# Scores of a latent-attention head in one product of 96 rows, the first projection by pairs of input chunks, and the last output tile by halves

## The reference

```python
h = h + 0.5 * SwiGLU_1(RMSNorm(h))            # width 2816
z = RMSNorm(h) @ w_in                         # 1824 columns
a = u * (W_s v + b)                           # chunk MLP
b = sliding-window attention with sinks       # 8 query heads, 2 key heads
c = latent attention, 4 heads                 # below
h = h + concat(a, b, c) @ w_out
h = h + 0.5 * SwiGLU_2(RMSNorm(h))
```

```python
s = q_nope . k_nope + q_pe . k_pe             # 64 terms + 32 terms, per head
p = softmax(s * (64 + 32) ** -0.5)            # masked by chunks of 64
```

## Time and profile before

| what | value |
|---|---|
| median of three runs | 2032.96 us |
| the profiled execution's own time | 2033.12 us |
| its span, first to last instruction | 2031.3 us |
| mean granted TensorE clock | 0.996 |
| PE busy | 2013.7 us, 99% |
| DVE, ACT, POOL busy | 1665.6, 972.5, 356.6 us |
| DMA over the span | 175.40 MB, 86 GB/s |

### The profile page before, as it was taken

How to read it: one execution, slowest core, us unless ns; L and a number is a source line. 1 busy time by engine, 2 the same in 40 slices (tenths; PEclk the granted TensorE clock), 3 DMA queues, 4 the chain that set the end, 5 groups by cost and what they waited for, 6 DMA issues and landing times.

```text
span 2031.3 us, 40732 instructions
## 1 busy us (share of the span) xinstructions
PE 2013.7 (99%) x15315; PEld 1961.2 (97%) x15315; DVE 1665.6 (82%) x2456; ACT 972.5 (48%) x1768; POOL 356.6 (18%) x218
## 2 busy tenths in 40 slices
PE   8999999999999999999999999999999999999998
PEld 7999999999889999999999999999987899999998
DVE  7999998755667999998689999976466599999975
ACT  6544453354546544453364444534546474444532
POOL 1222200042112222200012221002321213222000
PEclk8999999999999999999999999999999999999999
DMA  4323223342122232332222322324221123322321
GB/s 135 104 83 103 91 85 95 83 106 67 35 55 84 87 100 89 97 93 79 79 91 96 103 83 89 106 79 114 81 62 45 61 65 104 96 89 80 107 87 66
DMA packets 234855, 175.40 MB, mean 86 GB/s; under 512 B 35185, under 2 KB 231025, under 8 KB 234737
## 3 DMA queue, kind: packets, MB, share of 16 engines
q1 hardware_dynamic: 232624, 171.68, 28.3%
q10 hardware_dynamic: 2112, 2.10, 0.3%
HBM read 170.14 MB, written 3.62 MB: 86 GB/s over the span
## 4 chain that ended last, share of the span: by engine, by line
PE 94%; DVE 3%; ACT 2%; issue 1%; DMA 1%; ACTq 0%; DVEq 0%; SPq 0%
PE pair L1474 43%; PE pair L1423 32%; PE pair L1597 9%; PE pair L1530 2%; PE pair L1744 1%; PE pair L1724 1%; DVE t_parts L2067 1%; PE pair L1735 1%; PE pair L1730 1%; PE pair L1767 1%; PE pair L1752 1%; DMA x_tok<-in_x_prompt_dram 0%; ACT square L928 0%; PE pair L1760 0%; DVE t_parts L2350 0%
## 5 line engine op out<-in xcount | busy, mean ns | idle before, releaser
L1474 PE MATMUL pair<-t_parts,chunk_high 128*128 128x288 f32 x4480 | 893.5, 296 | 1.6 <-issue 1.2
L1474 PEld LDWEIGHTS pair<-t_parts,chunk_high 128*128 128x128 f32 x4480 | 719.5, 189 | 2.7 <-DVE chunk_low L2032 2.7
L1474 PE MATMUL pair<-t_parts,chunk_low 128*128 128x288 f32 x2240 | 661.6, 295 | 0.0
L1474 PEld LDWEIGHTS pair<-t_parts,chunk_low 128*128 128x128 f32 x2240 | 421.5, 188 | 0.0
L973 ACT ACTIVATE chunk_high<-chunk_sum 128x512 fp32r<-128x512 f32 x320 | 199.4, 631 | 380.4 <-DVE chunk_sum L2020 184.7
L870 POOL TENSOR_TENSOR chunk_low<-set_raw,chunk_high 128x512 fp32r<-128x512 f32 x160 | 229.4, 1443 | 716.4 <-ACT chunk_high L973 716.4
L864 POOL TENSOR_TENSOR w_low<-raw,w_high 128x1024 fp32r<-128x1024 f32 (+1 forms) x46 | 114.0, 2482 | 589.4 <-ACT w_high L921 589.4
L2032 DVE TENSOR_TENSOR chunk_low<-chunk_sum,chunk_high 128x512 fp32r<-128x512 f32 x320 | 207.1, 689 | 8.1 <-ACT chunk_high L973 0.5
L1423 PE MATMUL pair<-hidden_high,w_high 128*128 128x288 f32 x896 | 192.2, 296 | 0.0
L1423 PE MATMUL pair<-hidden_high,w_low 128*128 128x288 f32 x896 | 191.9, 296 | 0.0
L1423 PE MATMUL pair<-hidden_low,w_high 128*128 128x288 f32 x896 | 191.7, 296 | 0.0
(11 more groups left out here) (297 smaller groups left out, 3785.5 us busy)
## 6 DMA issues: line engine op xcount, KB each, us to landing
set_raw<-in_w_up_dram SPq DMA_DIRECT2D x44, 1024.0 KB, 5.4
set_raw<-in_w_gate_dram SPq DMA_DIRECT2D x44, 1024.0 KB, 5.4
raw<-in_w_down_dram SPq DMA_DIRECT2D x64, 448.0 KB, 3.6
down_raw<-in_w_down_dram SPq DMA_DIRECT2D x16, 1024.0 KB, 5.1
raw<-in_w_in_dram SPq DMA_DIRECT2D x20, 512.0 KB, 3.9
raw<-in_w_in_dram SPq DMA_DIRECT2D x16, 256.0 KB, 3.9
raw<-in_w_out_dram SPq DMA_DIRECT2D x8, 512.0 KB, 3.4
raw<-in_w_out_dram SPq DMA_DIRECT2D x16, 256.0 KB, 3.8
```

The source lines that it names most:

```text
L1474: mm = nc.tensor.matmul(out, c[:, j, p, :], tr[p // 2][:, seat(p), x, t, :], start=p == 0 and n == 0, stop=p == KP - 1 and n == 2)
```

## The change

Three edits are made together.

**Latent attention.** Keys and queries are kept per head: `kS[h]` and `qS[h]`, partitions 0-63 content, 64-95 rotary. A unit of MS is one product of 96 rows per head (for the sample queries two, cached and own keys). To fill these, `kn` is copied out in two copies of 64 partitions, `qn` in two on DVE, ACT copies the rotated queries to four heads at `A:1`, the cached rotary keys to four at `rot:kpe`, and the rotated keys from head 0 to three more at the end of `kn:0`. `PLAN` is unchanged.

**Opening.** The first gains (16 rows) are loaded and transposed ahead of x, the others later; the first up set comes in two DMAs of 512 KB after `x_in[0]` and `x_in[1]`; chunks 6 and 7 of x are transposed behind the first 12 matmuls, and the two tiles are made by pairs of chunks in an interleaved order; ACT rounds each tile's weights one pair of chunks earlier.

**End.** Chunk 7 is made first for columns 0-287, then for 288-575; in the middle of the second half PE sums and transposes the first two token tiles, whose scaling and stores then run early. The squares of chunk 7 go straight into the sum over channels.

```diff
+X_PAIR = [0, 1, 2, 3, 2, 3, 2, 3]
...
+        "MS": lambda: [scalar_ops(s)[-1] for s in ("kn:0", "kn:1", "A:1", "rot:kpe")],
         "kn": lambda: ["tc.0", "rkv.1"],
...
+        kS = [mix(f"keysT{j}", [P, KEYS]) for j in range(C_HEADS)]
+        qS = [mix(f"queriesT{j}", [P, NT]) for j in range(C_HEADS)]
...
+                if layer == 0 and w == 0:
+                    for n, signal in enumerate((first_in, set_in[0])):
+                        sp.wait_ge(x_in[n], 16)
+                        src = w_up[0].rearrange("(k p) n -> p k n", p=P)[:, :, n * P:(n + 1) * P]
+                        sp.dma_start(set_raw[0][:, :, :, n * P:(n + 1) * P].rearrange("p q e c -> p (q e) c"), src).then_inc(signal, 16)
+                    constants()
+                else:
+                    if w == 0:
...
-                    if p in (1, 2):
-                        free(p - 1)
-                        plain_chunks(q, 0, p - 1)
+                    n = p - chunk_after
+                    if n in (0, 1):
...
+                    act.wait_ge(gains_T, 2)
+                    nc.scalar.activation(gains[:, EARLY_ROWS:], ps[3][:, 1, EARLY_ROWS:N_GAINS], ACT.Copy).then_inc(gains_ready, 1)
                 root(ph, ps[3][:, 0, 0:QUARTER_T])
...
+                    if step == "A:1":
+                        dve_did(act, layer, "rot:qp.2")
+                        for h_ in range(C_HEADS):
+                            copy(qS[h_][ROPE], zs[1][32 * h_:32 * h_ + 32], f"{step}.{h_}")
+                        continue
+                    if step == "rot:kpe":
+                        for h_ in range(C_HEADS):
+                            copy(kS[h_][ROPE, NT:KEYS], ckpeT[ROPE], f"{step}.{h_}")
...
-                        copy(knT[arg][:, :], flat(p)[:, 0:KEYS], f"{step}.0")
+                        for j in range(2):
+                            copy(kS[2 * arg + j][NOPE], flat(p)[64 * j:64 * j + 64, 0:KEYS], f"{step}.{j}")
+                        if arg == 0:
+                            dve_did(act, layer, "rot:kpe.2")
+                            for h_ in range(1, C_HEADS):
+                                copy(kS[h_][ROPE, 0:NT], kS[0][ROPE, 0:NT], f"{step}.{1 + h_}")
                     elif kind in ("T", "MT"):
...
+
+                    for n, p in ((0, 0), (None, 6), (None, 7), (0, 1), (1, 0), (1, 1), (0, 2), (1, 2), (0, 3), (1, 3)):
+                        if n is None:
+                            x_transposes(p)
+                            continue
+                        if n == 0 and p == 0:
+                            pe.wait_ge(plain_low, 1)
+                        elif n == 1 and p == 0:
+                            pe.wait_ge(low_by_pool, 2)
+                        for e in range(2):
+                            if n == 0:
+                                for signal in (t_ready[B21],) if e else (t_ready[B11], b12_ready):
+                                    pe.wait_ge(signal, p + 1)
+                            mm = tile_part(0, n, 2 * p + e, e, p)
+                        if p == KP - 1:
+                            mm.then_inc(chunk_used, (3, 4)[n])
+
                 def plain_tile(b, n):
...
+                def plain_by_halves(m, between):
+
+                    for half in range(2):
+                        for n in range(2):
+                            s = base_slot + 2 * m + n
+                            low_in(layer, s)
+                            for i in range(DOWN_K):
+                                w_h, w_l, f_h, f_l = down_tile(s, i, down_first(2 * m + n) + i)
+                                for k, (c, x) in enumerate(((w_h, f_h), (w_h, f_l), (w_l, f_h))):
+                                    mm = nc.tensor.matmul(ps[DOWN_PAIR[m]][:, half, 0:HALF], c, x[:, half * HALF:(half + 1) * HALF],
+                                                          start=n == 0 and i == 0 and k == 0, stop=n == 1 and i == DOWN_K - 1 and k == 2)
+                            if half:
+                                release(mm)
+                            elif n:
+                                mm.then_inc(last_half, 1)
+                            if half and n == 0:
...
-                            r = slice(64 * j, 64 * j + 64)
-                            nc.tensor.matmul(ps[p][0:nq, j, 0:W], qnT[pair][r, t0:t0 + nq], knT[pair][r, SEQ:KEYS] if i == 4 else knT[pair][r, 0:W],
-                                             start=True, stop=False)
-                        for k_pe, at0, col, n in ((ckpeT, 0, 0, PAST), (kpeT, SEQ, PAST, DEC)) if i == 4 else ((kpeT, 0, 0, W),):
-                            for j in range(2):
-                                r = slice(32 * (2 * pair + j), 32 * (2 * pair + j) + 32)
-                                mm = nc.tensor.matmul(ps[p][0:nq, j, col:col + n], qpT[r, t0:t0 + nq], k_pe[r, at0:at0 + n],
-                                                      start=False, stop=col + n == W)
+                            h_ = 2 * pair + j
+                            for col, at0, n in ((0, NT, PAST), (PAST, SEQ, DEC)) if i == 4 else ((0, 0, W),):
+                                mm = nc.tensor.matmul(ps[p][0:nq, j, col:col + n], qS[h_][BOTH, t0:t0 + nq], kS[h_][BOTH, at0:at0 + n], start=True, stop=True)
...
+            def early_tokens():
+
+                pe.wait_ge(h_ready, last - 1)
+                pe.wait_ge(y_ready, KD - 1)
+                pe.wait_ge(last_h, 1)
+                pe.wait_ge(sq_added, 2 * KD * DEPTH)
+                pe.wait_ge(sq_made, last)
+                for t in range(2):
+                    square_sum(t, sq_sum, True, False)
+                    mm = square_sum(t, sq_tmp, False, True)
+                mm.then_inc(sum_done, 1)
+                pe.wait_ge(y_ready, KD)
+                for t in range(2):
+                    for m in range(KD):
+                        mm = y_chunk(t, m)
+                    mm.then_inc(y_done, 1)
 
...
-                    y_chunk(t, m)
-            pe.wait_ge(sq_added, 2 * KD * DEPTH + 1)
-
-            for t, (t0, n) in enumerate(TILES):
-                mm = nc.tensor.matmul(ps[3][0:n, 0, t:t + 1], sq_sum[:, t0:t0 + n], mean_d[:, 0:1], start=True, stop=True)
+                down(layer, 1, F2D, 2, early_tokens if layer + 1 == DEPTH else None)
+
+            for m in range(KD - 1):
+                y_chunk(2, m)
+            pe.wait_ge(root_done, 4 * DEPTH + 1)
+            pe.wait_ge(y_left, 2)
+            pe.wait_ge(y_right, 2)
+            for t in (2, 3, 4):
+                square_sum(t, sq_sum, True, False)
+            for m in range(KD - 1):
+                y_chunk(4, m)
+            pe.wait_ge(last_h, 2)
+            for m in range(KD // 2, KD - 1):
+                y_chunk(3, m)
+            pe.wait_ge(sq_made, last + 1)
+            for t in (2, 3, 4):
+                mm = square_sum(t, sq_tmp, False, True)
             mm.then_inc(sum_done, 1)
-            pe.wait_ge(y_ready, KD)
...
+                    if m == 3 and ph == 0:
                         plain_chunk_low(q, 0, 0)
...
-                        emit(nc.vector.tensor_tensor(dst[:, :], src[:, :], cos[:, :], ALU.mult), names[0])
                         pe_did(dve, layer, step)
+                        emit(nc.vector.tensor_tensor(src[:, :], src[:, :], cos[:, :], ALU.mult), names[0])
...
+            def last_update(half):
+                part, m = slice(half * HALF, (half + 1) * HALF), KD - 1
+                scratch = down_acc[:, half, :]
+                if half:
+                    slot_done(dve, DEPTH - 1, F2D + DOWN_SLOTS - 1)
+                else:
+                    dve.wait_ge(h_part, H_PARTS * ph + KD)
+                    dve.wait_ge(h_ready, last - 1)
+                    dve.wait_ge(last_half, 1)
+                nc.vector.scalar_tensor_tensor(out=scratch, in0=ps[DOWN_PAIR[m]][:, half, 0:HALF], scalar=0.5, in1=rms[:, part],
+                                               op0=ALU.mult, op1=ALU.mult).then_inc(out_scaled, 1)
+                dve.wait_ge(out_scaled, ph * KD + (m + 1 + half))
+                nc.vector.tensor_tensor(h[:, m, part], scratch, h[:, m, part], ALU.add).then_inc(last_h, 1)
+                dve.wait_ge(last_h, half + 1)
+                nc.vector.tensor_scalar(y_in[:, m, part], h[:, m, part], gain_of((DEPTH - 1) * KD + G_FFN1 + KD + m), None, ALU.mult).then_inc(y_ready, 1)
```

More of the change, by code:

```diff
@@ L1157, in tail @@
                     if layer + 1 == DEPTH:
-                        for m in range(4, KD):
+                        for m in range(4, KD - 1):
                             down_square(layer, 1, m)
@@ L1552, in release, with down @@
                 mm.then_inc(slot_used, 1)
-            def down(layer, w, base_slot, phase):
+            def down(layer, w, base_slot, phase, between=None):
                 ph = 2 * layer + w
@@ L1572, in plain @@
                         release(product(DOWN_PAIR[m], [down_tile(s, i, k0 + i) for i in range(DOWN_K)], first=n == 0, last=n == 1))
+                def plain_by_halves(m, between):
```

(34 more changed lines are left out.)

217 lines of the change are left out of this document (129 added, 88 removed).

## The result

The changed kernel takes 2041.16 us (median of 6 runs, 2039.88 to 2042.24), the kernel before 2033.41 beside it (2032.88 to 2034.56): ratio 1.0037, 95% interval 1.0026 to 1.0048. It is **slower by 7.75 us**; the prediction was 2031.2 us, with a range of 2025.5 to 2036.0. The profiled execution took 2040.92 us, of them 2039.1 in the span.

The account below looks back on a forecast made before the run. PE was taken to bound the middle of the kernel, but not its two ends. Attention +2.6, opening -2.6 and end -1.8 sum to -1.8 us: 2031.2 us, called "no change", range 2025.5 to 2036.

Parts of the forecast that it names:

- The walk of ACT's copies: Attention: added copies, 7.0 us a layer, followed through ACT's list to what PE waits for; 3.3 us late.
- T:9: Attention: PE's transposes of window unit 9, which wait for an ACT copy; forecast to start 3.3 us late.
- DVE's second query copy: Attention: 0.76 us, twice a layer, before things PE needs soon; taken to cost 0.35 each.
- The products' gain: Attention: products of 96 rows save 0.3 us in eight units and 0.15 in two, 2.7 us a layer.
- The rule of the packing: Attention, from the Trainium skill: row groups run concurrently, few rows take as long as full; 1.72 us either way, no gain.
- Rival 2: Attention: taller products gain nothing or lose by bare weight loads; put at 2039 us, chance 0.1.
- Rival 1: Attention: ACT's copies are hidden, so PE isn't late; -4.0 in place of +2.6, 2024.6 us, chance 0.2.
- The opening's term: Opening: PE starts at 13.9 us and ends the 96 matmuls at 30.1 instead of 32.7, -2.6 us.
- rival 3: Opening gives nothing, because the first landing or DVE's list ends last; 2033.8 us, chance 0.17.
- The first half set: Opening: first half of the up weights, issued at about 6 us, lands at 11.3 (bounds 9.5 and 13.5).
- DVE's gate part: Opening: the gate's first low part, next to be late, ready at 29.7 us; PE still finds it if unmoved.
- The end: Last tile by halves: path to the last scaling 9.0 against 9.6 us, store -1.2; together -1.8 us.

Follow-up runs that it names:

- the copies moved: The attention part alone with the same eleven rotary copies at other places in ACT's order: 2029.99 us, -3.9 against the kernel before.
- the filled waits: The attention part alone with two, one and two unused float32 products in three PE waits of each layer: 2039.03 us, +5.3 against the kernel before.
- The two runs that were to start or end them sooner: The opening part alone, with chunk 6's transposes ahead of PE's first twelve products: 2033.90 us; or with x's last 64 rows transferred first: 2034.68 us.

## Why the prediction was wrong, step by step

The sum had three terms. Attention was put at +2.6 us and measured +8.0 alone; the opening at -2.6 and measured +0.3; the end at -1.8 and measured -1.4. The first two failed.

**The walk of ACT's copies had the right mechanism and stopped one step early.** The prediction put T:9 3.3 us late, in front of it ACT's copies back to back, and that is what the trace has, only later. Two terms were too small and one was missing. (1) The copies: four of 576 columns on 32 partitions took 2.79 us, not 4 x 0.59, and two of 832 columns 1.75, not 1.52, twice; together 0.9 more. (2) DVE's second query copy cost 0.5 (PE waits 0.51 us for DVE at T:6; put at 0.35). 3.3 + 0.9 + 0.5 = 4.7; T:9 was 4.9 us late in the attention part alone (557.07 against 551.64, less the 0.5 by which that execution was late before the mixing). (3) Missing: **what the waiting does to PE's clock**. In the attention part alone T:9, the first unit and the next eight to twelve matmuls ran at 1.2 GHz. From T:9's start to the next transposes it takes 7.68 and 8.01 us in the two layers, where it takes 5.82 at the full clock with the copies moved, so 1.9 and 2.2 us a layer; the filled waits show 1.3 of it as time. The prediction took an idle PE as a loss of the idle time alone, although its own working had the half clock in the opening. 4.9 + 1.9 less the 2.8 of the products is +4.0. So a layer was +4.0 to +4.4 instead of +1.3: +8.0 in place of +2.6.

**The products' gain was right.** 2.7 us a layer were forecast. All latent scores' records of a layer, grouped by form, take 2.3 + 2.3 + 1.9 + 1.8 + 1.5 + 1.5 + 1.4 + 1.3 + 1.0 + 1.0 + 0.6 = 16.6 us before, the two largest being

```profile
L1730 PE MATMUL pair<-k_nopeT,q_nopeT 64*128 64x512 f32 x8 | 2.3, 641 | 0.0
L1735 PE MATMUL pair<-kpeT,q_peT 32*128 32x512 f32 x8 | 2.3, 640 | 0.0
```

and 3.9 + 3.0 + 2.3 + 2.2 + 1.3 + 1.1 = 13.8 with the taller products at the full clock, the largest being

```profile
L1756 PE MATMUL pair<-keysT,queriesT 96*128 96x512 f32 x8 | 3.9, 605 | 0.0
```

That is 2.8. These are lengths of overlapping records; by distances, from each unit's start to the same product five or six records behind it, the ten units save 2.6 us, from 0.05 to 0.5 each. A unit of 512 keys takes 1.92 us from its start to the next start (562.52 to 564.44), at the upper end of the 1.7 to 1.9 that the prediction named. The stage as a whole gives 1.7 to 1.9 us; 0.5 goes at T:6 and 0.4 to 0.5 in front of MS:1, where PE waits for DVE with its second copy, as here in the first layer with the copies moved:

```profile
560.17 1.10 PE L1756 MATMUL pair<-keysT,queriesT 96*128 96x256 f32 x4 [0.52 <-DVE queriesT L2514]
```

The rule of the packing, by which nothing would be gained, is refuted by a small margin, as the prediction had it. Rival 2 had the nearest time (2039), for a reason that doesn't hold: a unit does get shorter. Rival 1 was right that ACT has room for the copies, but not where the plan put them.

**The opening's term failed: -2.6 forecast, nothing measured** (rival 3, at a chance of 0.17). The first half set landed at 12.9, not 11.3; PE started at 15.6, not 13.9; its ten transposes of chunks 6 and 7, 1.97 us (1.9 forecast), now stood behind the start. Of the 2.6 us there were 0.8 when the 96 matmuls were done: the product after them starts at 32.97 in the opening part alone and at 33.79 before. In the kernel before PE comes to the first folded product (one whose weights are a sum of two chunks, `chunk_sum`) at 47.56 us,

```profile
47.56 0.43 PE L1474 MATMUL pair<-t_parts,chunk_high 128*128 128x288 f32 x2
```

and in the opening part alone 0.68 us sooner. But there it loses 0.7 us before the product at 50.73 and 0.3 before the one at 52.68, the 25th and the 37th of these:

```profile
46.88 0.42 PE L1494 MATMUL pair<-t_parts,chunk_high 128*128 128x288 f32 x2
...
50.73 0.50 PE L1494 MATMUL pair<-t_parts,chunk_high 128*128 128x288 f32 x2 [0.53 <-issue]
...
52.68 0.53 PE L1494 MATMUL pair<-t_parts,chunk_high 128*128 128x288 f32 x2
```

The second of them starts as soon as DVE has made the low part that it reads, in the chain of waits of this kernel

```profile
51.93 0.71 DVE chunk_low L2085
```

In every changed opening it starts some 0.05 us behind the end of that low part, which comes at 52.4 to 53.3 us; in the kernel before the low part ends at 52.22 and the product starts at 52.33 without a wait. The prediction held that the work of ACT and DVE on the chunks "now starts sooner" and would not bind. It started 0.6 us sooner (9.50 against 10.12), but it ended later: ACT's squares, the next thing on its list behind the last chunk's parts, start at 20.61 us before and in the changed kernel at

```profile
23.41 3.54 ACT L950 ACTIVATE square<-h 128x576 f32<-128x576 f32 x6
```

(22.89 in the opening part alone). On the way PE waited until 8.28 us for x's last rows, and ACT 1.97 us for chunk 6, which now stands behind the twelve matmuls; that these two are the whole reason is not shown. The prediction looked for the next bound at DVE's gate part near 30 us, where there was room, and not at these two lists as a whole, up to what PE asks of DVE at 52 us.

**The end was right:** -1.8 forecast, -1.6 in the trace, -1.4 alone, -0.9 behind the moved copies (-4.8 against -3.9). In the trace 1.0 of it is compute (0.6 forecast) and 0.6 the store (1.2), so the two parts were off by about the same amount in opposite directions, and that the sum is so near is luck.

The sum of what was measured, 8.0 + 0.3 - 1.4 = +6.9, leaves 0.8 of the 7.75, within the intervals. What stays open: whether the opening could give its 2 us if these lists ended sooner. The two runs that were to start or end them sooner hardly moved them, and none takes work off DVE.

## What to carry to other kernels

When work is added to an engine "with room", walk its list to the next thing that the bound engine waits for; the same eleven copies cost 8.0 us in one place and gave 3.9 in another. Copies that only a later unit reads go behind the earlier one. Where PE must wait for a few microseconds, price the time after the wait too. And before an early start is counted as a gain, ask when the other engines' lists end, not only what is late next.

## What was not expected of the hardware

- ACT copies of 32 partitions aren't shorter than those of 128: for 576 columns 0.70 us each from the rotated queries and 0.61 from head 0's keys (2.79 for four, 1.82 for three), where squares of 576 columns on 128 partitions take 0.59.
- Useless products make a kernel faster: five float32 ones in PE's waits of each layer, 2.6 us of extra work, keep the clock at 1.00 and take 2.7 us off the whole time.
- DVE's operation of 288 columns takes 2.28 us instead of 0.51 when GpSimd subtracts a whole chunk beside it (17.12 to 19.49). The Trainium skill names the cause ("GPSIMD Engine Reference", Key points: the two share their ways into the buffer, and DVE's instructions with two inputs there suffer); the trace agrees, with the second of these rows, beside the first, against the third:

```profile
17.12 2.37 POOL L913 TENSOR_TENSOR chunk_low<-set_raw,chunk_high 128x1024 fp32r<-128x1024 f32 x1 [16.67 <-ACT chunk_high L1198]
...
17.53 2.28 DVE L2487 SCALAR_TENSOR_TENSOR t_parts<-h,gains,t_parts 128x288 fp32r<-128x288 f32 x1
...
19.73 0.51 DVE L2487 SCALAR_TENSOR_TENSOR b<-h,gains,b 128x288 fp32r<-128x288 f32 x1
```
- Of the first two transfers behind the identity on one queue, the one issued second lets PE go only at about 8 us, whichever it is: x's last rows (256 KB) at 8.1 to 8.9, the gain rows (8 KB) at 7.9 to 8.1, which issued first are there at 5.0 to 5.3.
